# Sums of weight tiles for a seven-product scheme: from VectorE to accumulating transfers in device memory

## The reference, cut to what matters

```python
h = h + mixed @ w_out[l]
v = rms_norm(h, norm_ffn[l])
h = h + (jax.nn.silu(v @ w_ffn_gate[l]) * (v @ w_ffn_up[l])) @ w_ffn_down[l]
```

## Time and profile before

| | |
|---|---|
| median of 3 runs | 2855.72 us (2855.62 to 2856.9) |
| profiled execution | 2855.49 us, its span 2853.7 us |
| TensorE busy | 2847.0 us, 100% |
| VectorE busy | 2236.5 us, 78% |
| ScalarE busy | 1426.8 us, 50% |
| GpSimd busy | 66.5 us, 2% |
| DMA | 660.29 MB, mean 231 GB/s |

### The profile page before, as it was taken

The page is one execution under the profiler, slowest core; times in us unless marked ns, Lnnn a source line. Parts: engine busy times, 40 slices in busy tenths (PEclk is TensorE's granted clock), DMA queues, the critical chain, the costliest instruction groups (busy, mean ns, idle before and its releaser), DMA issues.

```text
span 2853.7 us, 32230 instructions
## 1 busy us (share of the span) xinstructions
PE 2847.0 (100%) x12714; PEld 2351.6 (82%) x12714; DVE 2236.5 (78%) x3139; ACT 1426.8 (50%) x1833; POOL 66.5 (2%) x115
## 2 busy tenths in 40 slices
PE   9999999999999999999999999999999999999999
PEld 7888888888888888888888888888888888888887
DVE  6887777788879877767787866576898887778877
ACT  5554455444544456554456665444454444554455
POOL 1000000000000000010001000000000000000000
PEclk9999999999999999999999999999999999999999
DMA  7555555555588868675555545555557986778966
GB/s 289 185 194 200 188 194 186 185 202 197 187 307 316 318 248 295 230 248 187 203 188 201 179 169 192 174 189 180 196 192 252 338 320 247 282 264 301 332 256 244
DMA packets 99096, 660.29 MB, mean 231 GB/s; under 512 B 11726, under 2 KB 11746, under 8 KB 25729
## 3 DMA queue, kind: packets, MB, share of 16 engines
q1 hardware_dynamic: 82224, 569.45, 57.2%
q10 hardware_dynamic: 12528, 76.08, 7.0%
q0 software_dynamic: 4192, 12.70, 1.3%
HBM read 620.42 MB, written 39.34 MB: 231 GB/s over the span
## 4 chain that ended last, share of the span: by engine, by line
PE 98%; DVE 1%; ACT 0%; issue 0%; DMA 0%; DVEq 0%; ACTq 0%
PE acc L768 93%; PE misc L768 5%; DVE w_lo L1674 0%; PE misc L773 0%; DVE heads_turned L1788 0%; ACT w_hi L1194 0%; DVE resid L1674 0%; DMA xT<-in_x_first 0%; ACT junk L1172 0%; DVE sum_out L1674 0%; ACT stage L1167 0%; DVE decay L1677 0%; DVE akT L1788 0%; DVE stats L2364 0%; DVEq L2426 0%
## 5 line engine op out<-in xcount | busy, mean ns | idle before, releaser
L1194 ACT ACTIVATE w_hi<-raw 128x1024 fp32r<-128x1024 f32 (+1 forms) x1014 | 1057.6, 1048 | 1064.0 <-PE acc L768 1023.0
L1674 DVE TENSOR_TENSOR w_lo<-raw,w_hi 128x1024 fp32r<-128x1024 f32 (+2 forms) x1016 | 1221.2, 1208 | 462.2 <-ACT w_hi L1194 454.6
L768 PE MATMUL acc<-w_hi,u_hi 128*128 128x512 f32 (+1 forms) x1472 | 581.2, 395 | 1.4 <-DVE w_lo L1674 1.1
L768 PE MATMUL acc<-w_hi,u_lo 128*128 128x512 f32 (+1 forms) x1472 | 571.0, 388 | 0.0
L768 PE MATMUL acc<-w_lo,u_hi 128*128 128x512 f32 (+1 forms) x1472 | 570.3, 387 | 0.0
L768 PE MATMUL acc<-w_hi,v_hi 128*128 128x512 f32 x1408 | 547.9, 389 | 0.0
L768 PE MATMUL acc<-w_hi,v_lo 128*128 128x512 f32 x1408 | 547.8, 389 | 0.0
L768 PE MATMUL acc<-w_lo,v_hi 128*128 128x512 f32 x1408 | 547.7, 389 | 0.0
L768 PEld LDWEIGHTS acc<-w_hi,u_hi 128*128 128x128 f32 x1472 | 276.9, 188 | 61.0 <-DVE w_lo L1674 3.5
L768 PEld LDWEIGHTS acc<-w_hi,u_lo 128*128 128x128 f32 x1472 | 276.7, 188 | 57.7
L768 PEld LDWEIGHTS acc<-w_lo,u_hi 128*128 128x128 f32 x1472 | 277.1, 188 | 55.3
(11 more groups left out here) (334 smaller groups left out, 2946.9 us busy)
## 6 DMA issues: line engine op xcount, KB each, us to landing
raw<-in_w_gates SPq DMA_DIRECT2D x112, 1024.0 KB, 4.8
raw<-in_w_ffn_gate SPq DMA_DIRECT2D x88, 1024.0 KB, 6.8
raw<-in_w_ffn_up SPq DMA_DIRECT2D x88, 1024.0 KB, 5.1
raw<-in_w_in SPq DMA_DIRECT2D x66, 1024.0 KB, 4.8
raw<-in_w_ffn_down SPq DMA_DIRECT2D x44, 1024.0 KB, 4.9
group_raw<-in_w_sums ACTq DMA_DIRECT2D x34, 1024.0 KB, 7.1
scratch_made<-group_raw ACTq DMA_DIRECT2D x34, 1024.0 KB, 8.1
raw<-in_w_out SPq DMA_DIRECT2D x32, 1024.0 KB, 4.8
```

The source lines that it names most:

```text
L768: return e.matmul(o, w, x, start=start, stop=stop, skip_group_check=True)
L1194: e.activation(m.w_hi[:, n % PART_SLOTS, 0:tiles * cols], m.raw_slot[slot][:, o * cols:(o + tiles) * cols], ACT.Copy).then_inc(s["w_hi_don ...
L1674: return e.tensor_tensor(o, a, b, op)
```

## The change

The task `group_sums` goes from all three engines, with its loads, its four additions and its stores. GpSimd gets a function of that name which makes a group within device memory. It copies `b11` into three quarters of `scratch_made` and `b22` into the fourth, then adds `b12` to all four, `b22` to two and `b21` to one by transfers with an accumulating write, each waiting until the one before has landed. Subtraction is not used, so the four sums are now `b11+b12`, `b11+b12+b22`, `b11+b12+b22+b21` and `b22+b12`; the signs of the left-hand sums and of three output steps change to suit.

GpSimd makes six groups after its first row scale, six after it has issued the load of `sums_all`, twelve (`f2hidden0`) after the row scale of the first feed-forward, ahead of the loads of the memory, and the last ten after the row scale of the second feed-forward. SyncE waits for `group_made` before it loads `scratch_made`, and, before it first uses the two extra slots in a down product, for the moves of earlier results (`MOVED_BEFORE`).

```diff
+MOVED_BEFORE = {"f1": NB, "f2": 4 * NB + sum(FF_PARTS)}
@@ walk, ffn
-            if ORDERS[mark][half]:
-                task(f"group_sums:{mark}{half}", f"{mark}hidden{half}")
...
-            if ORDERS[mark][half]:
-                lanes.finish(f"group_sums:{mark}{half}")
@@ load_chunk
         if plan.more_first.get(left) == c:
-            for g in plan.part_groups[left][-2:]:
-                e.wait_ge(s[f"group_stored{g % 2}"], 16 * (g // 2 + 1))
+            e.wait_ge(s["moved_lo"], MOVED_BEFORE[left[0:2]])
...
         if name == "scratch_made":
-            e.wait_ge(s[f"group_stored{b % 2}"], 16 * (b // 2 + 1))
+            e.wait_ge(s["group_made"], 16 * (b + 1))
@@ pool_program
+    def group_sums(groups):
+        for g in groups:
+            made, raw = (dram[n][g].rearrange("p (a b) -> p a b", a=CHUNK_KT) for n in ("scratch_made", "w_sums"))
+            b11, b22, b21, b12 = (raw[:, i:i + 1, :] for i in range(CHUNK_KT))
+            e.dma_start(made[:, 0:3, :], b11.to_broadcast([P, 3, BW])).then_inc(s["group_copied"], 16)
+            e.dma_start(made[:, 3:4, :], b22).then_inc(s["group_copied"], 16)
+            e.wait_ge(s["group_copied"], 32 * (g + 1))
+            e.dma_start(made, b12.to_broadcast([P, CHUNK_KT, BW]), accum_op=ALU.add).then_inc(s["group_added0"], 16)
+            e.wait_ge(s["group_added0"], 16 * (g + 1))
+            e.dma_start(made[:, 1:3, :], b22.to_broadcast([P, 2, BW]), accum_op=ALU.add).then_inc(s["group_added1"], 16)
+            e.wait_ge(s["group_added1"], 16 * (g + 1))
+            e.dma_start(made[:, 2:3, :], b21, accum_op=ALU.add).then_inc(s["group_made"], 16)
+            e.wait_ge(s["group_made"], 16 * (g + 1))
...
     row_root(0, m.r_mix)
+    n = len(plan.part_groups["f1hidden0"]) // 2
+    group_sums(plan.part_groups["f1hidden0"][:n])
     for h in range(4):
...
+    group_sums(plan.part_groups["f1hidden0"][n:])
     row_root(1, m.row_scale["f1"][0])
+    group_sums(plan.part_groups["f2hidden0"])
     for j in range(NB):
...
     row_root(5, m.row_scale["f2"][0])
+    group_sums(plan.part_groups["f2hidden1"])
@@ sum_left
-        tt(a21, a21, a22, ALU.add).then_inc(done, 1)
+        tt(a21, a21, a22, ALU.subtract).then_inc(done, 1)
...
-        tt(s4, a12, s2, ALU.subtract).then_inc(done, 1)
+        tt(s4, a12, s2, ALU.add).then_inc(done, 1)
@@ sums_out
-        tt(r12, r12, u1, ALU.add).then_inc(done, 1)
+        tt(r12, r12, u1, ALU.subtract).then_inc(done, 1)
         yield
-        tt(r22, r22, u3, ALU.add).then_inc(done, 1)
+        tt(r22, r22, u3, ALU.subtract).then_inc(done, 1)
         e.wait_ge(done, at("r22_u"))
-        tt(r22, r22, m5, ALU.subtract).then_inc(done, 1)
+        tt(r22, r22, m5, ALU.add).then_inc(done, 1)
```

More of the change, by code:

```diff
@@ L577 @@
     "w_hi_done", "w_lo_done", "half_read", "acc_freed0", "acc_freed1",
-    "group_landed0", "group_landed1", "group_made", "group_stored0", "group_stored1", "sum_left_made", "sums_copied", "sums_added",
+    "group_copied", "group_added0", "group_added1", "group_made", "sum_left_made", "sums_copied", "sums_added",
     "u_hi", "u_lo", "mem_hi", "mem_lo", "heads_squared", "heads_done", "moved_turned", "moved_hi", "moved_lo", "row_total", "row_root", "pool_scaled",
@@ L875, in evacuate @@
         pass
[L877 to L880, removed]
     def sums_out(b, j):
@@ L1150, in tensor_program @@
     work = {"x_move": x_move, "rows": rows, "first_out": first_out, "lam": lam, "keep_turn": keep_turn, "lru": lru, "diff": diff, "win": win, "fox_sums": fox_sums, "fox": fox, "gate_tanh": gate_tanh,
-            "mixed_move": mixed_move, "sums_out": sums_out, "group_sums": group_sums, "row_squares": row_squares, "resid_move": resid_move, "ffn_rows": ffn_rows,
+            "mixed_move": mixed_move, "sums_out": sums_out, "row_squares": row_squares, "resid_move": resid_move, "ffn_rows": ffn_rows,
             "hidden_move": hidden_move, "memory": memory, "final_rows": final_rows, "table": table, "norm": norm,
@@ L1519, in sums_out @@
         yield 2
[L1521 to L1541, removed]
     def memory():
```

## The result

The changed kernel takes 3011.99 us, median of 4 runs (3001.92 to 3017.64), against 2856.05 before: a ratio of 1.0542, 95% interval 1.053 to 1.0555, so 5.4% slower. The direction was forecast, the size was not: 2897.5 was predicted and 2965 was the upper end. The profiled execution has a span of 3015.8 us.

The account below looks back on a forecast made before the run. TensorE was taken as the bound, a queue of matmuls without gaps. A span of 2853.7 plus 36 us stall at memT plus 6 us in the down stages gave 2895.7, forecast as 2897.5 us; range 2853.5 to 2965.

Parts of the forecast that it names:

- The signs and the shifted small tasks: Changed additions and subtractions, and small tasks falling into other gaps: 0, the latter with a bound of 1 us either way.
- One sign that was named: VectorE's busy time should fall by 93 us in every case.
- The mechanism and its place: Third block's twelve groups delay memT's load in GpSimd's queue; ScalarE, VectorE, then TensorE wait: a stall of 36 us.
- the price of a group: GpSimd's copies and accumulating transfers for one group: 12.4 us of DMA engines, 35 us beside the stream, 19.2 us idle.
- The prediction's own bounds: DMA engine time of a group: 8.25 us if accumulating costs as much as copying, 13.5 us if it costs double.
- the formula: Group time beside the weight stream: engine time divided by the 0.44 left over, plus 6.8 us for four steps in series.
- The fixed part of a step: Each of a group's four serial steps has a fixed 1.7 us, taken from a 4 KB store; together 6.8 us.
- The first block: Six groups from 42.4 to 240.2 us, 33 us each available; at 35 they end 7 to 12 us late, costing 0.
- The stream in the down stages: Overbooked DMA engines delay weights in the two down stages: 3 us each, 6 together, bounds 0 and 14.
- Case 1: Accumulation no dearer than a copy, the chain fits everywhere below about 30 us a group: 2855 to 2861 us, chance 0.34.
- Case 3: A group takes over 40 us, possibly from slow descriptor writing beside VectorE; at 48 us about 3022 us, chance 0.19.
- case 4: Chain is fast, but its bursts delay single weight loads in the down stages: 7 to 20 us, about 2868, chance 0.04.

Follow-up runs that it names:

- e10: Kernel before the change with VectorE's 136 additions left out, each group loaded and stored as it is: 2855.65 us, ratio 0.9999.
- e3: Changed kernel with four instead of six groups before the differential heads and seven instead of twelve of f2hidden0 before the memory's loads: 2857.51 us, ratio 1.0006.
- e8: Kernel with both groups of moves (e3), but nine instead of seven groups of f2hidden0 before the loads of the memory: 2883.95 us.
- e5: Changed kernel with other tiles as sources, so that transfers have rows up to 8 KB instead of 2 KB throughout; same steps and bytes: 2904.52 us.
- e6: Changed kernel with two groups advanced together, each step issued for both before GpSimd waits once: 2947.85 us.
- e7: Changed kernel with six unread scaled copies per group added on VectorE during the gate and up stages: 3019.36 us.
- e9: Changed kernel with all its transfers, groups placed by the measured price, none before the scales of the differential heads: 2858.16 us, ratio 1.0007.

## Why the prediction was right and wrong

**What bounds the kernel: right.** TensorE had no gap, and freeing VectorE is worth 0 (e10: 2855.65 us). The signs and the shifted small tasks cost nothing that can be seen: with the groups in good places the whole change is at 2857.51 us (e3). One sign that was named failed: VectorE's busy time fell by 78 us and not by 93. The 93.2 us add up the records of the additions, and these overlap their neighbours by about 0.1 us each:

```profile
800.23 1.23 DVE L1674 TENSOR_TENSOR w_lo<-raw,w_hi 128x1024 fp32r<-128x1024 f32 x1 [0.95 <-ACT w_hi L1194]
801.37 0.69 DVE L1674 TENSOR_TENSOR group_raw<-group_raw 128x512 f32<-128x512 f32 x1
```

**The mechanism and its place: right.** The third block of twelve groups stands before the memory's load, ScalarE's queue stops at its wait for it, and w_hi, w_lo and TensorE stop in turn. The slack was counted as 31.7 us a group, with TensorE's prepared halves covering 6 us; e8 shows 6.6.

**The term that failed: the price of a group.** It was priced at 12.4 us of DMA engines, with 3.0 us a MiB copied and 1.8 times that for accumulated ones. Measured are 3.7 and a factor of 2.0, so 16.6 us. The prediction's own bounds, 8.25 to 13.5 us, did not hold it, because both ends rested on 3.0. That figure came from loads of long rows and small transfers; the repeated source tiles force rows of 2 KB, and with rows up to 8 KB the price is 13.7 us (e5). The factor was put at 1.8 because what a packet costs apart from its bytes would not double. For equal numbers of packets 1.8 was about right (e5), but accumulated rows of 2 KB went one to a packet and copied ones two. The Trainium skill (DMA: Bandwidth & Descriptors, SDMA does more than copy) calls the operation an elementwise reduction of two streams. Taken strictly, as the prediction's upper bound did, this would be double, and the measured 7.4 against 3.7 us agree.

**Beside the stream the formula held, with the idle engines it did not.** Engine time over the 0.44 that the stream leaves, plus 6.8 us, gives 44.5 us with 16.6 put in, and 44.4 was measured. For plain copies it gives 29.9 (measured 32.5), for long rows 37.9 (35.0), so it is good to 3 us. That is partly luck, as its 6.8 us is less than half of what a group costs beside its engine time when the stream stands. With the stream stopped it gives 23.4, and 31.8 was measured. The fixed part of a step was taken as 1.7 us, from a store of 4 KB. It is (31.8 - 16.6)/4 = 3.8 us for transfers of 80 to 528 packets, the second term of the sum that was mis-sized; what it consists of stays open (e6 saved only about half of it for each wait removed). Landing times in the changed kernel with the stream stopped, for the accumulating transfers of 1, 0.5 and 0.25 MiB (us, least, median, most):

```profile
DMA to landing us min/median/max: 10.5/10.6/10.7
DMA to landing us min/median/max: 6.9/7.1/8.2
DMA to landing us min/median/max: 4.6/4.7/5.0
```

Halving the size takes off a third.

**What followed.** By the same steps with the measured prices: in the third block 5.0 groups are done when the down stage begins and 3.3 more by the time ScalarE wants the memory. The 3.7 left at 31.8 us are 118 us, plus about 6 us for the load, less 6: 118 against a measured wait of TensorE of 112.1. The prediction had 36, since it had 1.9 groups left at 19.2 us. Of the 118 us, 3.7 x 8.4 = 31 come from the fixed part of the steps. The first block was put at 0, because 35 us a group used up just the slack; at 40.6 us it is 46 us late (286 instead of 240), less the 3 us until VectorE wants the scale and the 6 us prepared: 37, measured 37.6. Errors of 9 and 13 us in the price of a group (35 against 44 beside the stream, 19.2 against 31.8 with it stopped) thus became an error of 115 us. (The prediction's last sum is also 0.2 us short: 2895.7 + 1.8 + 0.2 is 2897.7.) Where a chain of twelve runs against a fixed date, its end moves by twelve times the error in one.

**The stream in the down stages: too high.** 6 us were counted for the two down stages. TensorE lost 2.0 us in the first (1046 to 1197) and 0.3 in the second (busy 119.69 of 120 us from 2540 on); the short waits added in the whole program are 5.8. The overbooked engines delay the groups, not the weights: TensorE was busy 149.01 of 151 us in the first at a share of 0.98.

**The rivals.** Case 1 (nothing waits) could not happen at these prices: its bound of 30 us a group lies below the 32.5 us of plain copies. Case 3 was the right one: it priced 48 us a group at about 3022 us, and 44.4 us gave 3012. It had been given 0.19 and most of it was left outside the range. Its possible cause, a busy VectorE, finds no support in e7; the causes are row length, the doubled accumulation and the steps' fixed part. The traffic as a cost of its own, case 4, measured 1.7 and 2.4 us (e3, e9), and both intervals include nothing and reach to 4.6.

## What to carry to other kernels

Before work is moved to a queue that is nearly idle, list what else stands in that queue, by when each item is wanted, and divide the time in between by the number of new items. The price of one item has to stand clear of that quotient, since an error in it is multiplied by the number of items. Where it doesn't fit, the order of the queue is the cheap remedy: moving seven groups recovered 154 of 156 us here, with no transfer changed. And work taken off an engine that does not make the bottleneck wait is worth nothing: here 136 additions, 78 us of VectorE.

## What the runs showed of the hardware

- Accumulating writes within device memory took twice the DMA engine time of plain copies of the same size: 7.4 against 3.7 us a MiB in rows of 2 KB. In rows of 2 KB the accumulating transfers put one row into a packet and the copies two; at equal packets, 0.5 MiB took 3.3 against 1.8 us.
- A transfer of 0.25 MiB that accumulates landed 4.7 us after its issue beside idle engines, one of 1 MiB after 10.6 us. A quarter of the bytes took nearly half the time.
- With two queues on full DMA engines (share 0.98), the weight stream of large rows kept its pace and the transfers of small rows slowed from 31.8 to 50.3 us a group. Whether row length or the number of loads in flight decides this is not shown.
- After the stop of 112 us, in which the granted clock fell to 0.50 (1.2 GHz), TensorE's first 14 matmuls came 0.43 us apart instead of 0.23, about 3 us lost (each lasted 0.63 us instead of 0.39). From 1345 us on the clock was 1.00 again. After the first long wait it went alike, and together this is most of the 6.6 us of added busy time:

```profile
1336.90 0.79 PE L785 MATMUL acc<-w_hi,v_hi 128*128 128x512 f32 x1 [112.11 <-DVE w_lo L1664]
1337.49 0.63 PE L785 MATMUL acc<-w_lo,v_hi 128*128 128x512 f32 x1
```

```profile
1328.00:1345.00 17.00, 8.10 (x23) 6.41 (x24) 8.93 (x11) 8.93 (x15) 3.27 (x6) 0.56 0.42 134
1345.00:1360.00 15.00, 15.00 (x68) 12.43 (x67) 9.60 (x13) 8.43 (x12) 0.00 (x0) 1.00 0.74 268
```
